# Rows of the normed activations padded to multiples of 64 bytes

## The reference, cut to what matters

```
D_MODEL = 1024; SEQ = 256
D_FF = -(-8 * D_MODEL // (3 * 256)) * 256        # 2816

def rmsnorm(x, g):
    y = x32 * lax.rsqrt(jnp.mean(x32 * x32, axis=-1, keepdims=True) + EPS)
    return y * g

def swiglu(h, w_gate, w_up, w_down):
    return (jax.nn.silu(h @ w_gate) * (h @ w_up)) @ w_down

def first_block(x, ...):
    for i in range(DEPTH):                       # DEPTH = 2
        h = rmsnorm(x, norm_mix[i])
        x = x + (conformer_conv(h, ...) if i % 2 == 0 else dilated_attention(h, ...))
        h = rmsnorm(x, norm_ffn[i])
        x = x + swiglu(h, ffn_w_gate[i], ffn_w_up[i], ffn_w_down[i])
    return rmsnorm(x, final_norm)

def second_block(x, c, ...):
    cond = jax.nn.silu(c)
    for l in range(DEPTH):
        sh1, sc1, g1, sh2, sc2, g2 = split(cond @ ada_w[l] + ada_b[l], 6)
        h = _rms_norm(x, norm_mix[l]) * (1.0 + sc1) + sh1
        x = x + g1 * (mixer(h, ...) @ w_out[l])
        h = _rms_norm(x, norm_ffn[l]) * (1.0 + sc2) + sh2
        x = x + g2 * _swiglu(h, ffn_gate[l], ffn_up[l], ffn_down[l])
```

## Time and profile before

| | us |
|---|---|
| median of three runs | 1253.21 |
| the profiled execution | 1253.02 |
| its span, first to last instruction | 1251.7 |
| TensorE matmul busy | 1191.0 (95%) |
| VectorE busy | 893.0 (71%) |
| ScalarE busy | 653.6 (52%) |
| mean granted TensorE clock | 0.990 of full speed |

### The profile page before, as it was taken

One profiled execution on the slowest core, in us unless ns is written; L12 is line 12 of the kernel. 1 busy time (PEld: TensorE's weight loads), 2 busy tenths in 40 slices (PEclk: granted clock), 3 DMA queues, 4 the chain that ended last, 5 costly groups with the idle time before them and its releaser, 6 DMA issues.

```text
span 1251.7 us, 22615 instructions
## 1 busy us (share of the span) xinstructions
PE 1191.0 (95%) x8954; PEld 1085.9 (87%) x8954; DVE 893.0 (71%) x1631; ACT 653.6 (52%) x1101; POOL 79.7 (6%) x91
## 2 busy tenths in 40 slices
PE   7988999999998999999997989999999889999999
PEld 7867788889987888789987779999999778999999
DVE  6637676768776867669799768988885666766653
ACT  6336644445455554445564766454454776544441
POOL 2011000001000100002100111000000222000000
PEclk9999999999998999999998999999999999999999
DMA  8952777768763587758843335887786432655552
GB/s 290 247 158 86 265 273 254 253 221 298 272 207 115 175 270 248 252 185 298 301 135 110 125 101 186 273 261 244 251 298 212 154 110 86 218 180 185 180 199 68
DMA packets 81406, 257.97 MB, mean 206 GB/s; under 512 B 9033, under 2 KB 22165, under 8 KB 81301
## 3 DMA queue, kind: packets, MB, share of 16 engines
q1 hardware_dynamic: 75540, 250.69, 59.4%
q10 hardware_dynamic: 5760, 5.83, 1.8%
HBM read 253.82 MB, written 2.67 MB: 205 GB/s over the span
## 4 chain that ended last, share of the span: by engine, by line
PE 74%; DVE 10%; ACT 5%; issue 4%; DMA 3%; ACTq 1%; POOL 1%; SPq 0%; DVEq 0%; POOLq 0%
PE ps L570 49%; PE ps L597 6%; PE ps L599 6%; PE ps L598 6%; DMA uscr<-U 3%; DVE wlo L1400 2%; ACTq L962 1%; DVE X L1406 1%; ACT whi L959 1%; PE ps L740 1%; PE ps L731 1%; PE ps L732 1%; PE ps L709 1%; PE ps L736 1%; DVE aacc L1406 1%
## 5 line engine op out<-in xcount | busy, mean ns | idle before, releaser
L959 ACT ACTIVATE whi<-raw 128x1024 fp32r<-128x1024 f32 (+1 forms) x364 | 382.6, 1054 | 362.6 <-PE ps L570 218.8
L1400 DVE TENSOR_TENSOR wlo<-raw,whi 128x1024 fp32r<-128x1024 f32 (+1 forms) x364 | 441.9, 1223 | 102.8 <-ACT whi L959 101.2
L570 PE MATMUL ps<-HH,whi 128*128 128x258 f32 (+1 forms) x1448 | 421.1, 291 | 16.5 <-DVE wlo L1400 7.8
L570 PE MATMUL ps<-HH,wlo 128*128 128x258 f32 (+1 forms) x1448 | 411.9, 284 | 0.0
L570 PE MATMUL ps<-HL,whi 128*128 128x258 f32 (+1 forms) x1448 | 411.4, 284 | 0.0
L570 PEld LDWEIGHTS ps<-HH,whi 128*128 128x128 f32 x1448 | 276.7, 191 | 30.8 <-issue 21.3
L570 PEld LDWEIGHTS ps<-HL,whi 128*128 128x128 f32 x1448 | 277.3, 192 | 0.4
L570 PEld LDWEIGHTS ps<-HH,wlo 128*128 128x128 f32 x1448 | 276.5, 191 | 0.0
L570 PE MATMUL ps<-GH,whi 128*128 128x256 f32 x704 | 195.9, 278 | 1.5 <-DVE sg L1406 1.0
L570 PE MATMUL ps<-GL,whi 128*128 128x256 f32 x704 | 195.0, 277 | 0.0
L570 PE MATMUL ps<-GH,wlo 128*128 128x256 f32 x704 | 195.0, 277 | 0.0
(11 more groups left out here) (253 smaller groups left out, 1115.1 us busy)
## 6 DMA issues: line engine op xcount, KB each, us to landing
raw<-wall SPq DMA_DIRECT2D x363, 512.0 KB, 4.3
araw<-ada SPq DMA_DIRECT2D x96, 512.0 KB, 4.7
UR<-uscr ACTq DMA_DIRECT2D x32, 142.0 KB, 3.7
oBB<-kbias SPq DMA_DIRECT2D x16, 192.0 KB, 2.5
aTB<-scratch SPq DMA_DIRECT2D x12, 128.0 KB
uscr<-U ACTq DMA_DIRECT2D x8, 143.5 KB, 4.4
out<-X SPq DMA_DIRECT2D x8, 128.0 KB, 2.9
aTB<-scratch SPq DMA_DIRECT2D x12, 64.0 KB
```

The lines of the kernel that those rows point to most:

```text
L570: ins = pe.e.matmul(o, l, r, start=(kt == p.order[0] and i == 0), stop=(kt == p.order[-1] and i == 2))
L959: ac.then_inc(ac.e.activation(o, i, func, **kw), sem)
L1400: dv.then_inc(dv.e.tensor_tensor(o, a, b, op), sem)
```

## The change

`HH` and `HL` get rows of TW = T + 16 = 272 words, 1088 bytes, which is 17 times 64: every row now starts at a multiple of 64 bytes. How many columns each matmul reads stays as it was, 256, 258 or pieces of 128; only the distance between rows is larger. `product_wide` and the `double` tiles read their stationary pieces from the same rows.

The four tiles take 4 · 8 · 56 = 1792 bytes per partition more. Room for it comes from `wdw` (992 bytes) leaving `vec`, and from `dist`, of which only the table in use is kept and loaded (1536 bytes less). `RC` grows from 2 to 8 words per row. What is declared after them moves: `sg` and `tmp` start at a multiple of 64 now and started 32 bytes past one; `GH` and `GL` start at a multiple of 64 as before, an even one now and an odd one before; `row`, `MOD` and other small tiles now start 32 bytes past a multiple of 64.

The order of the instructions is the same on every engine, except for one load of 192 KB (the second `dist` table) less on SyncE, and the second load of `vec` is 124 KB smaller.

```diff
 UW = T + 28
+TW = T + 16
 NB = P + T
...
 
-VECS = [("nm0", 8), ("nm1", 8), ("nf0", 8), ("nf1", 8), ("fin", 8), ("bp1", 16), ("wdw", 248),
+VECS = [("nm0", 8), ("nm1", 8), ("nf0", 8), ("nf1", 8), ("fin", 8), ("bp1", 16),
         ("bdw", 8), ("lng", 8), ("lnb", 8), ("bp2", 8), ("nm2", 16), ("nf2", 16), ("adab", 96),
...
 NROW = 4 * 64 + 16
-VEC_FIRST = VCOL["wdw"]
+VEC_FIRST = VCOL["bdw"]
 X_PARTS = ((0, 2), (2, 4), (4, 8))
...
         X = sb("X", [P, KD, T])
-        HH = [sb(f"HH{i}", [P, KD, T + 2], F32R) for i in range(2)]
-        HL = [sb(f"HL{i}", [P, KD, T + 2], F32R) for i in range(2)]
+        HH = [sb(f"HH{i}", [P, KD, TW], F32R) for i in range(2)]
+        HL = [sb(f"HL{i}", [P, KD, TW], F32R) for i in range(2)]
         RST = [sb(f"RST{i}", [P, T]) for i in range(2)]
...
         ident, ones, bones = sb("ident", [P, P]), sb("ones", [P, P]), sb("bones", [P, P])
-        dist = sb("dist", [P, 2, 384])
+        dist = sb("dist", [P, 384])
         vec, row = sb("vec", [P, NVEC]), sb("row", [P, NROW])
...
         TMP = [SG[i // 2][:, i % 2 * T:i % 2 * T + T] for i in range(4)] + [sb(f"tmp{i}", [P, T]) for i in range(4, 9)]
-        RC = sb("rc", [P, 2, 2])
+        RC = sb("rc", [P, 2, 8])
         TN = [sb(f"tn{i}", [P, T]) for i in range(2)]
...
                 if i in FFN_NORM[:2]:
-                    act(RC[:, FFN_NORM.index(i), :], bank[7][:, 0:2], ACT.Sqrt, S.sd, bias=epsb[:, 0:1], scale=1.0 / D)
+                    act(RC[:, FFN_NORM.index(i), 0:2], bank[7][:, 0:2], ACT.Sqrt, S.sd, bias=epsb[:, 0:1], scale=1.0 / D)
                     return
...
                         dv.wait_ge(S.sd, NORM_RST[i] + 1)
-                        dv.then_inc(dv.e.reciprocal(RC[:, f, :], RC[:, f, :]), S.rst)
+                        dv.then_inc(dv.e.reciprocal(RC[:, f, 0:2], RC[:, f, 0:2]), S.rst)
                     if s >= 8 and s % 8 == 0:
...
                         if k == 0:
-                            dv.wait_ge(S.kdist, 32)
-                            ts(eDS[:, :], dist[:, 0, :], 1e20, -1e30, ALU.is_ge, ALU.mult, S.top)
+                            dv.wait_ge(S.kdist, 16)
+                            ts(eDS[:, :], dist[:, :], 1e20, -1e30, ALU.is_ge, ALU.mult, S.top)
                             dv.settle()
...
                         dv.settle()
-                        tt(eDS[:, :], eDS[:, :], dist[:, 0, :], ALU.add, S.sel)
+                        tt(eDS[:, :], eDS[:, :], dist[:, :], ALU.add, S.sel)
                     if what in ("dscore", "sscore", "dfact", "sfact"):
...
             load(row[:, :], row_in, S.row)
-            for i in range(2):
-                load(dist[:, i, :], kdist[i], S.kdist)
+            load(dist[:, :], kdist[0], S.kdist)
             load(wq[:, :, :], wq_in, S.wq)
...
     vec = np.concatenate([cols(v) for v in (
-        I["norm_mix"], I["norm_ffn"], I["final_norm"], I["conv_b_pw1"], I["conv_w_dw"], I["conv_b_dw"],
+        I["norm_mix"], I["norm_ffn"], I["final_norm"], I["conv_b_pw1"], I["conv_b_dw"],
         I["conv_ln_g"], I["conv_ln_b"], I["conv_b_pw2"], I["norm_mix_2"], I["norm_ffn_2"], I["ada_b_2"],
...
```

## The result

The changed kernel is a little slower: the median of 11 runs is 1265.90 us (1261.24 to 1272.51), against 1253.36 us for 11 runs of before; the ratio is 1.0095, with a 95% interval of 1.0071 to 1.0120. The forecast of 1225 us, its range and its sign were wrong. The span of the profiled execution went from 1251.7 to 1262.3 us at the same granted clock (0.990 and 0.991).

The account below looks back on a forecast made before the run. The pitch of TensorE's matmuls was taken to bound the kernel. Gains of 6.2 + 0.7 + 6.0 + 12.9 + 2.6 = 28.4 us off 1253.02 us gave 1225 us, range 1212 to 1245.

Parts of the forecast that it names:

- rival D: In HH, the start of a row is not the cause; nothing changes, 1252 to 1253 us; chance 0.09.
- Term 5: The rest: moved small tiles and smaller loads, dn0 to dn3 unchanged, dn2 1.5 us either way; all counted at nothing.
- rival E: GH and GL, moved to even multiples of 64, slow dn0 to dn3 to 117.8 ns: 1265 us; chance 0.05.
- Terms 1 and 2: Matmuls with 256 moving columns of HH fall to 113.3 ns, 6.2 us; mixd's double tiles likewise, 0.7 us.
- Term 3: Wide products, 1056 matmuls, go from 232.4 to 226.7 ns: 6.0 us, ends 0 and 13.1 us.
- Term 4: 258 moving columns go from 120.2 to 114.1 ns: 12.9 us in gu2 and gu3, 2.6 us in mixe and mixo.
- rival B: 258-column matmuls stay as they are, since 1032 bytes always touch 17 pieces of 64 bytes: 1240.1 us; chance 0.25.
- Rival C: Aligned rows run at the slow pace, 117.8 ns for 256 columns, no wide gain: 1247 us; chance 0.10.

Follow-up runs that it names:

- gh_fine: Changed kernel with GH and GL rows 72, 80, 96 and 112 bytes past the weights' place modulo 256 in dn0 to dn3: 1260.57 us, one run.
- gh64: Changed kernel with 64 unused bytes ahead of GH, so GH and GL lie 64 bytes past the weights' place modulo 256: 1260.31 us, ratio 1.0045.
- rows_odd: Changed kernel with HH and HL rows of 1152 bytes, at distances alternating between 64 and 192, and GH at 64: 1260.17 us, ratio 1.0026.
- before_gh64: Kernel before with 64 unused bytes ahead of GH, which gives GH distance 0; HH rows stay unpadded: 1269.71 us, ratio 1.0097.
- nudge64: gh64 with one small matmul, its result unread, after tiles 2 to 6 of each of dn0 to dn3: 1258.78 us.
- gh64_again: The same program as gh64, run a second time: 1260.53 us.
- dense: Changed kernel with HH and HL rows of 1024 bytes, 1056 for 258 columns; every 256-column row at distance 192: 1248.21 us, ratio 0.9952.
- dense_again: The same program as dense, run again: 1249.31 us, ratio 0.9929.

## Why the prediction was wrong, point by point

**What bounds.** Right. The matmul pitch sets the time: 12.4 us more in the pitches, 3.7 less and 2.1 us of idle time gave the 10.6 us of span, and every experiment on `GH` moved the time the same way.

**The premise, that start alignment to 64 bytes makes the quick pace.** Wrong, and by size the larger failure: terms 1 to 4 rest on it, forecast 28.4 us and brought 3.7. It was read from two streams, `GH` at 113.3 ns and `HH` at 118.5, which also differed in distance. `gh_fine` has 113.4 ns 48 bytes further than `gh64`, where the rows aren't aligned, and `gh64` 117.8 in aligned rows. The rows that should have warned were quoted: `dn2`, aligned, at 117.8 ns, and kt = 0, aligned, no quicker than its neighbours. Against rival D I wrote that nothing else differs between `mixd` and `dn0` but tile and row; their addresses did.

**Term 5, "`dn0` to `dn3` have their rows as before: 0".** This is the step that turned the sign. The change moves `GH` from an odd to an even multiple of 64, as rival E itself says, and I priced the move at nothing: it cost 12.4 us. I took the shape of the rows for the whole of their layout.

**Terms 1 and 2, 6.9 us.** Measured 1.4: no product fell to 113.3; `mixd` went from 118.4 to 118.1 by starts, the double tiles from 118.4 to 118.0, and `pw1`, `outd`, `oute` and `outo` lost 1.0 to 1.6 ns. Padding had replaced one mixture of distances by another. **Term 3, 6.0 us.** Measured 1.4 ns, 1.5 us; the 226.7 ns that I took do exist, of the places tried at distance 0 alone. **Term 4, 15.5 us.** Measured 0.8: `gu3` x838 in 100 us against x836. Here rival B was right in its number: `gu2` and `gu3` had 119.7 to 120.5 ns with every layout tried. Its reason, a price of a seventeenth piece of 64 bytes on top of 113.3 ns, isn't what the runs show: in the same rows 256 columns have 117.8 ns in `rows_odd` and 118.3 in after, so that the two further columns cost 2.4 and 1.5 ns and not 7.1. The match of 120.4 with 120.2 was luck. B's time, 1240, missed as well, since it kept terms 1 to 3.

**Rival E.** It named what did it, the move of `GH` to an even multiple of 64 from the weights, and the time, 1265, which was measured. That two reads meet there, its reason, is not shown: the runs show that the distance counts, not how. Its prices weren't right: it wanted 117.8 ns in `dn0` and the wide matmuls above 237, and it was 120.0 and 231.0. The chance of 0.05 was too low, since the only fact against it was the premise above; and since a second slow value (120) was not thought of, its sum was right by luck, two errors that cancel: 8.0 us for `GH`, which cost 12.4, and 5.3 us for the wide products, which gained 1.5. Rival C's pace, 117.8, is a real state of streams at distances 64 and 192. Rival D was right that the start of a row isn't the cause, and wrong in its time, because `GH` moved.

**The notes.** By the row, the same 256 columns cost 113.3 to 122.0 ns by placement and pace alone, at granted clock 1.00. The Trainium skill, page "TensorE: Matmul & The Clock Gate", section "Back-to-back issue gap", has no term for placement in N/2.4 + 2.5, so by it the change does nothing; the runs disagree by 1%. The page gives that formula for a matmul by itself and not for a stream of them, which the prediction left out. The estimate of 115.1 ns from its page "Advanced Engine Details and Errata", section "SBUF Cachelines", isn't borne out either: 258 aligned columns had 119.7.

## What to carry to other kernels

Where a stream of matmuls sets the time, look at where its two operands lie relative to each other, not only at each one's alignment, and treat a change of any buffer's size as a change of the place of all that follow it. Keep the addresses of hot tiles fixed with a gap when sizes change; here 704 bytes of gap turned a loss of 1% into a gain of 0.4%. Compare the mean granted clock of two kernels before a difference of a few us is put down to the change. When two streams differ in pitch, list everything that differs between them before one cause is priced over thousands of instructions.

## What the runs showed of the hardware that was not expected

- At full clock the pitch of 256 columns of float32r, with a weight load for each, depends on the distance modulo 256: 0: 120.0 ns; 16, 32: 116.7; 48: 118.3; 64: 117.8 or 113.4; 72: 120.1 to 122.0; 80: 118.3; 96: 120.0; 112: 113.4; 128, 144, 160: 118.7; 176: 119.3; 192: 117.8 or 113.4; 208: 119.2; 240: 117.2. That 256 is the period rests on little: `GH` lies 768 bytes further from the weights in `before_gh64` than in after, with 120.0 ns in both. A period of 128 has against it 120.0 at 0 and 118.7 at 128, and 113.4 at 112 and 117.2 at 240. All distances but 0, 64, 112 and 192 were seen in one product of one execution each, so a second pace there isn't ruled out.
- Two paces at one place (`nudge64`, `gh64` against `gh64_again`, `dense` against `dense_again`), kept for hundreds of matmuls or switched by one small matmul.
- Open: why these distances, what in the start picks the pace, and whether distance 112 for the 256-column streams with distance 0 for both wide products would bring what their pitches promise. That kernel was not tried.
